# Output stage of a hybrid encoder: gain applied by GpSimd, last norm applied per token in the PSUM copies, four output buffers, a new order of rows in the stores

## The reference, cut to what matters

```python
for i in range(DEPTH):                       # DEPTH = 2
    h = h + mixer_i(rmsnorm(h, norm_mix[i]))
    h = h + swiglu(rmsnorm(h, norm_ffn[i]), ffn_w1[i], ffn_w3[i], ffn_w2[i])
return rmsnorm(h, norm_final)[:, N_META:]    # x * rsqrt(mean(x*x) + 1e-6) * g, per token
```

## Time and profile before

| what | value |
|---|---|
| time, median of 3 runs | 3051.34 us (3047.39 to 3055.39) |
| the profiled execution's own time | 3048.04 us |
| its span, first to last instruction | 3046.2 us |
| mean granted TensorE clock | 0.97 of full speed |
| TensorE busy in the span | 2850.6 us, 94% |
| last addition to `h` begins | 2982.16 us |
| first store of the output is issued | 3014.33 us |

### The profile page before, as it was taken

How to read it: one execution, slowest core, us unless ns; L and a number is a source line. 1 busy time by engine, 2 the same in 40 slices (tenths; PEclk the granted TensorE clock), 3 DMA queues, 4 the chain that set the end, 5 groups by cost and what they waited for, 6 DMA issues and landing times.

```text
span 3046.2 us, 40610 instructions
## 1 busy us (share of the span) xinstructions
PE 2850.6 (94%) x15387; PEld 2355.0 (77%) x15387; DVE 1296.7 (43%) x1638; ACT 642.7 (21%) x1109; POOL 1348.3 (44%) x1390
## 2 busy tenths in 40 slices
PE   5999999999999999999995899998799999999994
PEld 5888887899999999998883444443578888888882
DVE  3444444352222222227466566665352222233335
ACT  3333433310000000002000555543210000000001
POOL 3565555344444444445231455554344444444440
PEclk8999999999999999999997799999899999999996
DMA  6222223211111111113111000000311111111111
GB/s 186 60 72 55 65 64 136 98 48 42 50 46 46 49 46 44 44 44 123 53 53 74 22 22 15 36 15 11 144 45 49 49 46 47 45 45 46 50 45 59
DMA packets 230023, 174.15 MB, mean 57 GB/s; under 512 B 25912, under 2 KB 210912, under 8 KB 229232
## 3 DMA queue, kind: packets, MB, share of 16 engines
q1 hardware_dynamic: 218320, 130.99, 15.0%
q10 hardware_dynamic: 11552, 41.02, 3.6%
HBM read 139.90 MB, written 32.53 MB: 57 GB/s over the span
## 4 chain that ended last, share of the span: by engine, by line
PE 82%; DVE 10%; issue 3%; DMA 2%; SPq 1%; ACT 1%; ACTq 0%; POOL 0%; DVEq 0%; POOLq 0%
PE PS L631 58%; PE PS L756 8%; PE PS L973 3%; DVE nmx L1635 2%; PE PS L985 2%; PE PS L807 2%; PE PS L843 2%; PE PS L783 2%; DVE rcp L1678 2%; PE PS L931 1%; PE PS L906 1%; PE PS L664 1%; DMA out<-fin 1%; DVE accd L1665 1%; DVE ssq L1352 1%
## 5 line engine op out<-in xcount | busy, mean ns | idle before, releaser
L457 POOL TENSOR_TENSOR wh<-wraw,ones 128x512 fp32r<-128x512 f32 (+1 forms) x456 | 416.0, 912 | 1249.8 <-PE PS L631 1077.5
L460 POOL TENSOR_TENSOR wl<-wraw,wh 128x512 fp32r<-128x512 f32 (+1 forms) x456 | 514.8, 1129 | 35.8
L631 PE MATMUL PS<-uh,wh 128*128 128x348 f32 (+1 forms) x1760 | 451.8, 354 | 17.1 <-DVE h L1388 5.9
L631 PE MATMUL PS<-ul,wh 128*128 128x348 f32 (+1 forms) x1760 | 447.2, 352 | 0.0
L631 PE MATMUL PS<-uh,wl 128*128 128x348 f32 (+1 forms) x1760 | 445.7, 351 | 0.0
L1388 DVE TENSOR_TENSOR h<-PS,h 128x1044 f32<-128x1044 f32 (+1 forms) x192 | 236.9, 1234 | 331.8 <-PE PS L631 317.0
L631 PEld LDWEIGHTS PS<-uh,wh 128*128 128x128 f32 x1760 | 310.9, 190 | 53.9 <-DVE h L1388 7.0
L631 PEld LDWEIGHTS PS<-ul,wh 128*128 128x128 f32 x1760 | 312.4, 189 | 31.9
L631 PEld LDWEIGHTS PS<-uh,wl 128*128 128x128 f32 x1760 | 311.8, 189 | 30.4
L631 PE MATMUL PS<-yh,wh 128*128 128x348 f32 x1056 | 225.4, 322 | 6.0 <-DVE h L1388 6.0
L1073 ACT ACTIVATE at<-at 128x1044 f32<-128x1044 f32 (+1 forms) x44 | 47.1, 1070 | 864.4 <-DVE at L1400 864.4
(11 more groups left out here) (203 smaller groups left out, 4094.2 us busy)
## 6 DMA issues: line engine op xcount, KB each, us to landing
wraw<-in_ffn_w SPq DMA_DIRECT2D x176, 256.0 KB, 2.9
wraw<-in_ffn_w SPq DMA_DIRECT2D x176, 128.0 KB, 2.2
wraw<-in_a_w_qkv SPq DMA_DIRECT2D x48, 256.0 KB, 2.9
biasb<-bias_rows SPq DMA_DIRECT2D x256, 36.0 KB, 1.9
h<-h_spill ACTq DMA_DIRECT2D x16, 522.0 KB, 9.1
qkv_spill<-tq ACTq DMA_DIRECT2D x12, 522.0 KB, 2.7
h_spill<-h SPq DMA_DIRECT2D x8, 522.0 KB, 10.6
h_spill<-h ACTq DMA_DIRECT2D x8, 522.0 KB, 3.2
```

Of the source, the lines that this page charges most:

```text
L457: nc.gpsimd.tensor_tensor(wh[:, slot, 0:w], wraw[:, slot, 0:w], ones[:, 0:1].to_broadcast([P, w]), ALU.mult).then_inc(s_whi, 1)
L460: nc.gpsimd.tensor_tensor(wl[:, slot, 0:w], wraw[:, slot, 0:w], wh[:, slot, 0:w].bitcast(F32), ALU.subtract).then_inc(s_wrd, 1)
L631: mm = nc.tensor.matmul(PS[:, set_ + c, 0:cw], w, x[k][:, c * cw:(c + 1) * cw], start=(first and i == 0 and ti == 0), stop=(last and i == ...
```

## The change

The gain is no longer applied together with `rstd`. GpSimd multiplies each chunk of `h` with its gains when the addition to that chunk is done, into a new tile `hg`, and writes it in another order of tokens inside each block: column by column (c, r) where `h` has (r, c). ScalarE writes the squares in this order too. The statistic of a token is made on that token's partition: 8 products with the 128 columns of `ssq` as weights and one column of ones give a tile of 128x8, and mean, root and Newton step are made on it. The transposes read `hg`; the two copies out of PSUM multiply with the token's scalar. There are four pairs of PSUM banks and four `fin` buffers in place of one pair and two buffers. The view of the output in the store is now 16 (columns), 8 (rows), 1024. A dummy Sqrt loads ScalarE's table ahead of the real one. `fin` shares its memory with tiles of the FFN that are dead by then.

```diff
+OUTS = 4
+F_BANK = [(6, 7), (5, 2), (0, 1), (3, 4)]
@@ SyncE
-                sp.dma_start(out_g[i % 2, :, CB * (i // 2):CB * (i // 2) + CB, :],
-                             fin[:, i % 2, :]).then_inc(s_out[i % 2], 16)
+                sp.dma_start(out_g[i % 2, :, CB * (i // 2):CB * (i // 2) + CB, :].rearrange("r c d -> c r d"),
+                             fin[:, i % OUTS, :]).then_inc(s_out[i % OUTS], 16)
@@ GpSimd, after split_ffn(1); by_row and by_column view a chunk as p, i, r, c
+            for m in range(KC):
+                po.wait_ge(s_df, G_FF[1] + 125 + m)
+                nc.gpsimd.tensor_scalar(by_column(hg[:, m, :]), by_row(h[:, m, 0:GRID]), gains[:, 4, m:m + 1], None,
+                                        ALU.mult).then_inc(s_hg, 1)
@@ TensorE
-            stat(4)
+            pe.wait_ge(s_ssq, 4)
+            pe.wait_ge(s_df, G_FF[1] + 132)
             for i in range(8):
-                pe.wait_ge(s_fs, KC * (i // 4 + 1))
+                mm = nc.tensor.matmul(PS[:, 4, i:i + 1], ssq[:, P * i:P * i + P], ones[:, 0:1],
+                                      start=True, stop=True)
+            mm.then_inc(s_st, 1)
+            pe.wait_ge(s_hg, KC)
+            for i in range(8):
+                if i == 3:
+                    pe.wait_ge(s_fv, 1)
+                if i >= 4:
+                    pe.wait_ge(s_fca, i - 3)
+                    pe.wait_ge(s_fcb, i - 3)
                 for f in range(2):
-                    if i:
-                        pe.wait_ge(s_fcb if f else s_fca, i)
                     for c in range(4):
-                        mm = nc.tensor.transpose(PS[:, 6 + f, P * c:P * c + P],
-                                                 h[:, 4 * f + c, P * i:P * i + P], ident[:, :])
+                        mm = nc.tensor.transpose(PS[:, F_BANK[i % 4][f], P * c:P * c + P],
+                                                 hg[:, 4 * f + c, P * i:P * i + P], ident[:, :])
                     mm.then_inc(s_ft, 1)
@@ ScalarE
+                if k == 4:
+                    nc.scalar.activation(by_column(buf[:, m % 2, 0:t]), by_row(h[:, m, 0:t]),
+                                         ACT.Square).then_inc(s_sq, 1)
...
+            nc.scalar.activation(sst[:, 8:9], ones[:, 0:1], ACT.Sqrt).then_inc(s_rt, 1)
+            act.wait_ge(s_fv, 1)
+            nc.scalar.activation(ssy[:, 0:8], ssv[:, 0:8], ACT.Sqrt).then_inc(s_rt, 1)
+            act.wait_ge(s_rs, 5)
             for i in range(8):
                 act.wait_ge(s_ft, 2 * i + 1)
-                if i >= 2:
-                    act.wait_ge(s_out[i % 2], 16 * (i // 2))
-                nc.scalar.activation(fin[:, i % 2, 0:512], PS[:, 6, :], ACT.Copy).then_inc(s_fca, 1)
+                if i >= OUTS:
+                    act.wait_ge(s_out[i % OUTS], 16 * (i // OUTS))
+                nc.scalar.activation(fin[:, i % OUTS, 0:512], PS[:, F_BANK[i % 4][0], :], ACT.Copy,
+                                     scale=ssv[:, i:i + 1]).then_inc(s_fca, 1)
@@ VectorE
+            dve.wait_ge(s_st, 5)
+            nc.vector.tensor_scalar(ssv[:, 0:8], PS[:, 4, 0:8], 1.0 / D, EPS, ALU.mult, ALU.add).then_inc(s_fv, 1)
+            dve.wait_ge(s_rt, 6)
+            refine(ssv[:, 0:8], ssy[:, 0:8], sst[:, 0:8], 4 + NG).then_inc(s_rs, 1)
             dve.wait_ge(s_rs, 5)
-            for half in (slice(0, GRID // 2), slice(GRID // 2, GRID)):
-                for m in range(KC):
-                    nc.vector.scalar_tensor_tensor(h[:, m, half], h[:, m, half], gains[:, 4, m:m + 1],
-                                                   rstd[:, half], op0=ALU.mult,
-                                                   op1=ALU.mult).then_inc(s_fs, 1)
             for i in range(8):
                 dve.wait_ge(s_ft, 2 * i + 2)
-                nc.vector.tensor_copy(fin[:, i % 2, 512:1024], PS[:, 7, :]).then_inc(s_fcb, 1)
+                nc.vector.tensor_scalar(fin[:, i % OUTS, 512:1024], PS[:, F_BANK[i % 4][1], :], ssv[:, i:i + 1], None,
+                                        ALU.mult).then_inc(s_fcb, 1)
```

More of the change, by code:

```diff
@@ L153, in build @@
             with ExitStack() as st:
+                with ExitStack() as st2:
+                    fin = sb("fin", [P, OUTS, D], F32, st2)
                 at1 = sb("at1", [P, 2, TP], F32, st)
-                gh1 = sb("gh1", [P, 2, 2, TP], F32R, st)
-                gl1 = sb("gl1", [P, 2, 2, TP], F32R, st)
+                gh_odd = sb("gh_odd", [P, 2, TP], F32R, st)
+                gl_odd = sb("gl_odd", [P, 2, TP], F32R, st)
+                gh_even = sb("gh_even", [P, 2, TP], F32R, st)
+                gl_even = sb("gl_even", [P, 2, TP], F32R, st)
                 sqf1 = sb("sqf1", [P, 2, TP], F32, st)
-                fin = sb("fin", [P, 2, D], F32, st)
+                hg = sb("hg", [P, KC, GRID], F32, st)
             with ExitStack() as st:
@@ L169, in build @@
             u_hi, u_lo = [uh, yh, uh, uh], [ul, yl, ul, ul]
-            gh = [[uh[:, 6:8, :], uh[:, 4:6, :]], [gh1[:, 0, :, :], gh1[:, 1, :, :]]]
-            gl = [[ul[:, 6:8, :], ul[:, 4:6, :]], [gl1[:, 0, :, :], gl1[:, 1, :, :]]]
+            gh = [[uh[:, 6:8, :], uh[:, 4:6, :]], [gh_even, gh_odd]]
+            gl = [[ul[:, 6:8, :], ul[:, 4:6, :]], [gl_even, gl_odd]]
         with ExitStack() as st:
@@ L260, in build @@
         s_or = sem("o_ready")
-        s_fs = sem("final_scaled")
+        s_hg = sem("final_gain_applied")
+        s_fv = sem("final_mean_made")
         s_ft = sem("final_transposed")
@@ L264, in build, with by_column, by_row @@
         s_fcb = sem("final_bank7_copied")
-        s_out = [sem(f"out_stored_from_buffer{i}") for i in range(2)]
+        s_out = [sem(f"out_stored_from_buffer{i}") for i in range(OUTS)]
+        def by_column(ap):
+            return ap.rearrange("p (i c r) -> p i r c", r=HR, c=CB)
+        def by_row(ap):
+            return ap.rearrange("p (i r c) -> p i r c", r=HR, c=CB)
         U_NA, U_WO, U_FF, U_GQ = 0, [48, 264], [64, 280], 240
@@ L443, in _ @@
                 sp.wait_ge(s_fcb, i + 1)
-                sp.dma_start(out_g[i % 2, :, CB * (i // 2):CB * (i // 2) + CB, :],
-                             fin[:, i % 2, :]).then_inc(s_out[i % 2], 16)
+                sp.dma_start(out_g[i % 2, :, CB * (i // 2):CB * (i // 2) + CB, :].rearrange("r c d -> c r d"),
+                             fin[:, i % OUTS, :]).then_inc(s_out[i % OUTS], 16)
             for stored in s_out:
-                sp.wait_ge(stored, 16 * 4)
+                sp.wait_ge(stored, 16 * 8 // OUTS)
         @block.gpsimd
@@ L1053, in squares @@
                 t = TOK[k // 3]
-                nc.scalar.activation(buf[:, m % 2, 0:t], h[:, m, 0:t], ACT.Square).then_inc(s_sq, 1)
+                if k == 4:
+                    nc.scalar.activation(by_column(buf[:, m % 2, 0:t]), by_row(h[:, m, 0:t]),
+                                         ACT.Square).then_inc(s_sq, 1)
+                else:
+                    nc.scalar.activation(buf[:, m % 2, 0:t], h[:, m, 0:t], ACT.Square).then_inc(s_sq, 1)
                 if k < 4:
@@ L1084, in ffn @@
                         act.dma_start(h_spill[:, m, :], h[:, m, :]).then_inc(s_hsp, 16)
-                root(2 * l + 2)
+                if l == 0:
+                    root(2)
             def proj_out(l):
@@ L1430, in ffn @@
                 add_square(k, KC - 1, sq_ffn[l])
-                rsqrt(k, sq_ffn[l])
+                if l == 0:
+                    rsqrt(k, sq_ffn[l])
             def proj_out(l):
@@ L1703, in _ @@
             ffn(1)
+            dve.wait_ge(s_st, 5)
+            nc.vector.tensor_scalar(ssv[:, 0:8], PS[:, 4, 0:8], 1.0 / D, EPS, ALU.mult, ALU.add).then_inc(s_fv, 1)
+            dve.wait_ge(s_rt, 6)
+            refine(ssv[:, 0:8], ssy[:, 0:8], sst[:, 0:8], 4 + NG).then_inc(s_rs, 1)
             dve.wait_ge(s_rs, 5)
-            for half in (slice(0, GRID // 2), slice(GRID // 2, GRID)):
-                for m in range(KC):
-                    nc.vector.scalar_tensor_tensor(h[:, m, half], h[:, m, half], gains[:, 4, m:m + 1],
-                                                   rstd[:, half], op0=ALU.mult,
-                                                   op1=ALU.mult).then_inc(s_fs, 1)
             for i in range(8):
                 dve.wait_ge(s_ft, 2 * i + 2)
-                if i >= 2:
-                    dve.wait_ge(s_out[i % 2], 16 * (i // 2))
-                nc.vector.tensor_copy(fin[:, i % 2, 512:1024], PS[:, 7, :]).then_inc(s_fcb, 1)
+                if i >= OUTS:
+                    dve.wait_ge(s_out[i % OUTS], 16 * (i // OUTS))
+                nc.vector.tensor_scalar(fin[:, i % OUTS, 512:1024], PS[:, F_BANK[i % 4][1], :], ssv[:, i:i + 1], None,
+                                        ALU.mult).then_inc(s_fcb, 1)
 def tables():
```

## The result

The changed kernel takes 3031.09 us (median of 7 runs, 3027.96 to 3038.27), the kernel before on the same chips 3049.66 us (7 runs, 3044.50 to 3055.39): a ratio of 0.9941, 95% interval 0.9930 to 0.9952. It is faster, as forecast, but by 18.6 us where about 35 were forecast, and 3031 lies above the stated range, which ended at 3028.

A forecast was written before the change was run, and what follows sets the result against it. The matmul stream bounds the kernel (TensorE busy 94%); only the 64.0 us tail, norm and then stores, can move. Span 3046.2 to 3011.6, 34.6 us less; 3016.7 by the runs' median, given as 3015, range 3006 to 3028.

The forecast's parts named there:

- the price of GpSimd's multiplies: Multiplies into `hg`: 1.9 us each, 15.2 us for eight, bounded by 1.04 and 2.37 us each.
- the forecast's mechanism: Tail: statistic and scalar hidden behind `hg`, ready at 2994.3; stores on 16 engines; span 3011.6 us; chance 0.62.
- B: Rival: GpSimd's strided write much slower, 3.8 us a multiply, `hg` ready at 3009.5, end about 3030; chance 0.12.
- A: Rival: GpSimd quicker, about 1 us a multiply, transposes begin behind the statistic at 2989.0, 3010 us; chance 0.12.
- C: Rival: output stores stay on half the engines, spacing 3.56 us, about 3032 us; chance 0.10.
- D: Rival: slower than before, the multiply becomes the whole tail, 6.35 us or more each; chance 0.02.
- E: Rival: no gain where it is meant, slow GpSimd and stores on half the engines together; chance 0.02.
- GpSimd's start: Multiplies begin only after GpSimd's last weight split, at 2978.07; TensorE waits for all eight before its first transpose.
- Contention: VectorE's additions of squares beside GpSimd's multiplies: loss between 0 and 3.7 us, taken as 1 us.
- The statistic and scalars: Norm: statistic 3.1 us, mean, root and Newton step with hops 1.7 us, done at 2990.7, hidden behind `hg`.
- The stores: Output loop: new view uses 16 engines for 8; seven spacings 11.1 us, last landing 3.1 us; four buffers suffice.
- TensorE's clock: Output transposes start at 1.2 GHz, 1.94 us a block, and may reach 2.4 GHz after 3.5 us of unbroken work.

The follow-up runs named there:

- two-tensor variant: The changed kernel with all eight GpSimd multiplies written as a product of two tensors, gain broadcast, same strided order: 3017.88 us, ratio to before 0.9900.
- row-order run: The changed kernel with tokens left in row order: multiplies and squares written without a stride, stores with the view of before: 3033.18 us, ratio to before 0.9952.
- the split of the work: The changed kernel with multiplies of chunks 0 to 4 on ScalarE, 5 to 7 on GpSimd, squares written without a stride: 3011.27 us, ratio to before 0.9881.

## Why the prediction was right in direction and wrong in size

**The step that failed** is the price of GpSimd's multiplies: "That is the nearest row in kind (a multiplication, one real tile), and I take 1.9 us for the strided write: 15.2 us." The row was a two-tensor product, the added instruction has the scalar form. For the two-tensor form the price was good: 1.91 and 2.03 us. The form in the change takes 2.84 us without the stride and 3.73 with it; eight took 30.8 us. The upper bound was at fault too: 2.37 us, an addition of two tiles, was taken as the dearest that one tile and a scalar could be. No row gave the price of the scalar form, for the kernel before had none on GpSimd. Nor was 2.37 us its slowest row: 16 additions of the same size took 2.94 us in the mean, which the prediction passes over. At that price eight would make 23.5 us, still short of 30.8.

```profile
L583 POOL TENSOR_TENSOR accp<-pf 128x1024 f32<-128x1024 f32 x16 | 47.0, 2937 | 188.9 <-ACT pf L1305 188.9
```

Two of the prediction's own signs of being wrong came true: multiplies of 3 us or more, and copies that wait for stores again.

Term by term, from the start of the last addition to `h`: `hg` ready after 12.1 us by forecast, 26.8 measured, 14.7 too few; from there to the end 17.3 by forecast, 18.3 measured, 1.0 too few. Together that is the difference of the tails, 29.4 to 45.1. With the two-tensor form the forecast's mechanism stands nearly by itself (34.0 us); of the 4.6 us that are left, 3.2 are in the time to `hg`, which is the contention, and 1.4 behind it.

**The rivals.** B came true almost to the number (3.8 us a multiply, about 3030), but its reason was mostly wrong: the stride gives 0.9 us of it, the form the rest. It held 12 in 100, and the range stopped inside it; priced as "no row shows this form", it deserved more and the range should have reached it. That it came out at 3030 is partly luck: the number was twice the price, whatever the reason. A, C, D and E fell.

**GpSimd's start.** Right: the multiplies began right behind the last split (2977.06), with TensorE waiting for all eight.

**Contention.** 1 us was taken of 0 to 3.7; the first multiply took 4.89 us, later ones 3.83, the sum of the eight is about 1 us over eight times 3.73. Right for this kernel, whose VectorE was nearly done, and too low for the two-tensor variant, where 3 us were lost. The Trainium skill (SBUF — State Buffer, "Who interferes with whom") says that a VectorE instruction with two SBUF inputs and a GpSimd instruction that reads SBUF exclude each other for a whole instruction. The rows of the two-tensor run agree, with 2.99 against 2.03 us, and 1.86 against 0.17 for a 128x8 product that ended with the multiply beside it. The changed kernel, with the scalar form, agrees only in part. Its first multiply lost 1.06 us to an addition already running, and an addition begun 0.4 us after the second multiply took 1.79 us. But the next addition, begun 2.6 us after that multiply, took its usual time:

```profile
2982.22 1.79 DVE L1390 TENSOR_TENSOR ssq<-ssq,sqf 128x1024 f32<-128x1024 f32 x1
2984.44 1.23 DVE L1390 TENSOR_TENSOR ssq<-ssq,sqf 128x1024 f32<-128x1024 f32 x1 [0.43 <-ACT sqf L1083]
```

So it is over the runs: VectorE's waits ended about 1 us after a scalar-form multiply began, in all cases but one, though it ran for 2.8 to 3.8 us. Why, no run shows.

**The statistic and scalars.** 3.1 us forecast, 3.57 measured; 1.7 and 1.7. Right, and hidden. The squares with the stride took 2.06 to 2.36 us against 1.06, the doubling that was given as the far end, and hidden as well. The copies with a scalar took 0.69 and 0.75 us on ScalarE and VectorE, 0.60 and 0.69 without, where the forecast had the scalar at nothing; either is short beside the stores' spacing of 1.4 us.

**The stores.** Right: the view sets the rate, shown in both directions (share 0.44 to 0.72 with two buffers, by the view alone; 0.79 back to 0.44 with four, where the strides changed as well). That it is 16 engines against 8 the packets bear out: besides 1024 packets of 4 KB the eight stores carry 64 small ones in the kernel before and in the row-order run, and 128 in every profile with the new view (here the changed kernel, with one packet of instructions besides). That is 8 and 16 a store, as one closing packet for each engine would give.

```profile
DMA packets 1153, 4.20 MB, mean 116 GB/s; under 512 B 128, under 2 KB 128, under 8 KB 1152
```

The Trainium skill (DMA: Bandwidth & Descriptors, "How many engines (k)") would have 8 and 16 for the two views; the shares of 0.44 and 0.99 agree. First store to end was forecast as 14.5 us, measured 15.4, and partly by luck: the seven spacings took 9.9 us, not 11.1, and the last store 5.5 us to the end, not 3.4. One store with others in flight landed after 4.9 us (median), not 3.1, so "four buffers suffice" was not quite so: ScalarE's copies waited 3.5 us in all for stores to land. The DMA engines were at a share of 0.99 meanwhile, so it is open whether a fifth buffer would have gained anything.

**TensorE's clock.** It stood at 0.50 while TensorE idled, and the transposes began there:

```profile
3011.00:3012.00 1.00, 1.00 (x6) 1.00 (x5) 0.35 (x1) 0.48 (x1) 0.00 (x0) 0.50 0.00 0
3012.00:3013.00 1.00, 1.00 (x8) 1.00 (x7) 0.40 (x1) 0.50 (x1) 0.00 (x0) 0.57 0.96 201
3013.00:3014.00 1.00, 1.00 (x12) 1.00 (x11) 0.75 (x1) 0.56 (x2) 0.00 (x0) 1.00 0.89 283
```

After some 5 us of transposes without a gap it was at the upper level, 2.4 GHz, where the forecast had 3.5, and a window of 1 us then touches 12 transposes in place of 6. A block of eight took 1.71 us at the lower level and 0.87 at the upper one. The forecast's 1.95 us a block was too high for the first, and its 1.3 was never the transposes' but the stores' bound.

**Where the gain lies.** The view by itself gives 10.4 us. Two more buffers give 5.5 us on top of it in the changed kernel. The new norm gives the rest of the 18.9 us, 3 us, where the split of the work shows 18 more to be had: GpSimd's multiplies fill the time that the scalings and the wide Newton step had taken. The split between view, buffers and norm is a difference of tails of single profiles, and the parts depend on each other, so it is good to a microsecond or two.

## What to carry to other kernels

A price is taken from a row of the same instruction form, not of the same arithmetic; where the form has no row in the trace, the far end of the range has to be wider than the neighbours' spread, and a rival that rests on such a price deserves a large share. When an engine is given work that others wait for as a whole, multiply its price by the count and set the end beside what else is ready: here the scalars were ready at 2991.0 and eight multiplies ran on until 3007.9. When stores run at a share near one half, look at the first dimension of their view before adding buffers.

## What the runs showed of the hardware that was not expected

- On GpSimd, for 128x1024 float32 without VectorE's additions beside it: copy 1.03 us, copy with a written stride of 8 elements 2.01; product with a broadcast, two-tensor form, 1.91 and 2.03; scalar form 2.84 and 3.83 with a scalar from memory, 2.78 and 3.74 with a constant. The stride costs a copy a whole microsecond and the two-tensor form next to nothing.
- The jump of the scalar form lies between written steps of 8 and 16 bytes (2.89 and 3.79 us); reading with a step of 64 bytes costs the same 0.8 us.
- Writing with a stride of 32 bytes took ScalarE 2.06 to 2.44 us for 1.04 to 1.16, and VectorE 2.00 us for 1.22 in an addition.
- A VectorE operation of 8 elements a partition took up to 1.97 us for 0.17 beside GpSimd's two-tensor multiplies; beside the scalar form it took at most 1.05, and in the changed kernel 0.17 to 0.38.
